# GpSimd finishes the normalised x of the plain feed-forwards, VectorE makes its low halves, and four pairs of columns run on the raw x in place of six

## The reference

```
def swiglu(x, w1, w3, w2):
    return (jax.nn.silu(x @ w1) * (x @ w3)) @ w2

x = layer_norm_2(DEEPNORM_ALPHA * x + mix, ln1_g[i], ln1_b[i])
x = layer_norm_2(DEEPNORM_ALPHA * x + swiglu(x, ffn_w1[i], ffn_w3[i], ffn_w2[i]), ln2_g[i], ln2_b[i])
```

## Time and profile before

| | |
|---|---|
| Median of three runs | 1377.0 us |
| The profiled execution | 1375.53 us |
| Its span, first to last instruction | 1373.7 us |
| TensorE matmul busy | 1355.4 us, 99% |
| VectorE busy | 978.7 us, 71% |
| ScalarE busy | 935.3 us, 68% |
| GpSimd busy | 423.4 us, 31% |
| Mean granted TensorE clock | 0.996 |

### The profile page before, as it was taken

How to read it: one execution, slowest core, us unless ns; L and a number is a source line. 1 busy time by engine, 2 the same in 40 slices (tenths; PEclk the granted TensorE clock), 3 DMA queues, 4 the chain that set the end, 5 groups by cost and what they waited for, 6 DMA issues and landing times.

```text
span 1373.7 us, 30422 instructions
## 1 busy us (share of the span) xinstructions
PE 1355.4 (99%) x11052; PEld 1320.7 (96%) x11052; DVE 978.7 (71%) x1523; ACT 935.3 (68%) x1597; POOL 423.4 (31%) x426
## 2 busy tenths in 40 slices
PE   9999999999999999999999999999999999999998
PEld 8899889999999999999999889999998989999998
DVE  7867776886548878875579868554587876855457
ACT  5633447756876577666977868457877897755876
POOL 3343002432203335322146028332044402632203
PEclk9999999999999999999999999999999999999999
DMA  5532205556564564565645235655644614666562
GB/s 212 175 116 92 86 32 183 168 184 200 177 196 157 183 203 137 181 200 191 198 157 187 74 128 170 209 192 167 215 151 150 216 61 153 208 193 194 186 201 93
DMA packets 63166, 225.74 MB, mean 164 GB/s; under 512 B 7008, under 2 KB 8416, under 8 KB 63072
## 3 DMA queue, kind: packets, MB, share of 16 engines
q1 hardware_dynamic: 62064, 221.47, 50.3%
q10 hardware_dynamic: 1008, 3.01, 0.6%
HBM read 223.40 MB, written 1.05 MB: 163 GB/s over the span
## 4 chain that ended last, share of the span: by engine, by line
PE 82%; DVE 9%; ACT 5%; issue 2%; DMA 1%; POOL 0%; SPq 0%; DVEq 0%; ACTq 0%; POOLq 0%
PE bank L486 21%; PE bank L487 21%; PE bank L507 15%; PE bank L615 6%; DVE w_lo_space L1970 2%; ACT w_hi_space L1285 1%; PE bank L535 1%; PE bank L549 1%; PE bank L523 1%; DVE both L2074 1%; PE bank L481 1%; PE bank L483 1%; PE bank L482 1%; PE bank L1027 1%; PE bank L1020 1%
## 5 line engine op out<-in xcount | busy, mean ns | idle before, releaser
L1970 DVE TENSOR_TENSOR w_lo_space<-raw,w_hi_space 128x1024 fp32r<-128x1024 f32 x294 | 381.5, 1305 | 99.5 <-ACT w_hi_space L1285 92.0
L1285 ACT ACTIVATE w_hi_space<-raw 128x1024 fp32r<-128x1024 f32 x298 | 312.3, 1052 | 80.9 <-PE bank L507 50.5
L486 PE MATMUL bank<-x_hi,w_hi_space 128*128 128x262 f32 (+6 forms) x1144 | 286.4, 287 | 0.5 <-DVEq L2077 0.5
L487 PE MATMUL bank<-x_lo,w_hi_space 128*128 128x262 f32 (+6 forms) x1144 | 283.1, 284 | 0.0
L1968 DVE SCALAR_TENSOR_TENSOR w_lo_space<-raw,negmean,w_hi_space 128x1024 fp32r<-128x1024 f32 x120 | 158.0, 1317 | 145.4 <-ACT w_hi_space L1283 145.0
L486 PEld LDWEIGHTS bank<-x_hi,w_hi_space 128*128 128x128 f32 x1144 | 216.9, 190 | 1.9 <-issue 1.1
L487 PEld LDWEIGHTS bank<-x_lo,w_hi_space 128*128 128x128 f32 x1144 | 217.0, 190 | 0.3
L486 PE MATMUL bank<-x_space,w_hi_space 128*128 128x256 f32 (+3 forms) x896 | 214.9, 280 | 0.0
L487 PE MATMUL bank<-x_space,w_hi_space 128*128 128x256 f32 (+3 forms) x896 | 214.1, 280 | 0.0
L2884 POOL TENSOR_TENSOR a_space<-av,a_space 128x256 fp32r<-128x256 f32 (+1 forms) x88 | 99.5, 1131 | 309.0 <-ACT a_space L1543 124.5
L486 PEld LDWEIGHTS bank<-x_space,w_hi_space 128*128 128x128 f32 x896 | 169.2, 189 | 0.1
(11 more groups left out here) (516 smaller groups left out, 2691.8 us busy)
## 6 DMA issues: line engine op xcount, KB each, us to landing
raw<-w SPq DMA_DIRECT2D x418, 512.0 KB, 3.8
h<-h SPq DMA_DIRECT2D x4, 272.0 KB, 3.8
out<-h SPq DMA_DIRECT2D x8, 128.0 KB, 1.9
T<-cs ACTq DMA_DIRECT2D x1, 960.0 KB, 6.4
con_b<-cb ACTq DMA_DIRECT2D x1, 712.0 KB, 6.1
con_g<-ca ACTq DMA_DIRECT2D x1, 421.5 KB, 6.2
p_raw<-pin ACTq DMA_DIRECT2D x1, 256.0 KB, 3.5
smx<-pin ACTq DMA_DIRECT2D x1, 256.0 KB, 6.4
```

The costliest lines, as they stand in the source:

```text
L486: pe.matmul(o, wh, xh, start=first, stop=False)
L487: pe.matmul(o, wh, xl, start=False, stop=False)
L1285: A(weights_of(s)[0][:, slot, :], raw[:, slot, :], ACT.Copy).then_inc(S("hi_ready"), 1)
L1970: V.tensor_tensor(wl[:, slot, :], raw[:, slot, :], wh[:, slot, :].bitcast(F32), ALU.subtract).then_inc(S("lo_ready"), 1)
```

## The change

`RAW_PAIRS` goes from 6 to 4. GpSimd no longer makes the low halves of the normalised x; it finishes `h` itself, with `keep` (a multiplication by `rstd`, a wait for its own result, then one instruction with gain and bias), for all eight tiles before it comes to the hidden values. ScalarE takes its rounded half as a plain copy of the finished `h`, two tiles in pair 0, three in pair 1, three in pair 2, and no longer makes the full one. VectorE makes the low halves, in the same places, behind the `av` of the pair. The feed-forwards with a convolution keep their code. `keep` was in the program and is:

The diff:

```
--- before.py
+++ after.py
@@ -82,7 +82,7 @@
 
 X2_STEP = KT * SEQ
 
-RAW_PAIRS = 6
+RAW_PAIRS = 4
 RAW_CONV = 10
 
 NEXT_LINE = [U["up2"] + 2 * RAW_PAIRS, U["up3"] + 2 * RAW_PAIRS, U["m_out"]]
@@ -345,6 +345,10 @@
         def x2_low(i, k):
 
             return x2[:, k, halves_x[i]:2 * halves_x[i]] if i < 2 else x2_late[1][:, k, :]
+
+        def late_tiles(j):
+
+            return (range(0, 2), range(2, 5), range(5, 8))[j] if j < 3 else ()
 
         def a_tile(i, part, j, n):
 
@@ -1588,7 +1592,10 @@
                     act.wait_ge(S("unit_done"), u + 2)
                     ahead(u + 1, s + 1)
                     if conv is None:
-                        tiles = range(2 * j, min(2 * j + 2, KT))
+                        for k in late_tiles(j):
+                            act.wait_ge(S("ln_h"), KT * 2 * ups[0] + k + 1)
+                            A(x2_high(ups[0], k), h[:, k, 0:N], ACT.Copy).then_inc(S("x2_hi"), 1)
+                        tiles = ()
                     else:
                         tiles = range(2) if j == 0 else range(j + 1, min(j + 2, KT))
                     for k in tiles:
@@ -2428,6 +2435,10 @@
 
                     dve.wait_ge(S("a_ready"), j + (base + 1))
                     V.scalar_tensor_tensor(out=av[:, par, 0:M], in0=gate[:, N - M:N], scalar=gate[:, N:N + 1], in1=sl[:, par, 0:M], op0=ALU.add, op1=ALU.mult).then_inc(S("ffn_product"), 1)
+                    if conv is None:
+                        for k in late_tiles(j):
+                            dve.wait_ge(S("x2_hi"), KT * ups[0] + k + 1)
+                            V.tensor_tensor(x2_low(ups[0], k), h[:, k, 0:N], x2_high(ups[0], k).bitcast(F32), ALU.subtract).then_inc(S("x2_ready"), 1)
 
                 one_over(2 * ups[0], N)
                 if conv is None:
@@ -2865,7 +2876,8 @@
                     centre(c, j, N)
 
             def low_parts(i, n, N, M):
-                kept[0] += 1
+                if i < 2:
+                    kept[0] += 1
 
                 def times(k):
                     G.tensor_tensor(h[:, k, 0:N], r[:, k, 0:N], rstd[:, 0:N], ALU.mult).then_inc(S("ln_h1"), 1)
@@ -2875,17 +2887,18 @@
                     pool.wait_ge(S("ln_h"), KT * n + k + 1)
                     G.tensor_tensor(x2_low(i, k), h[:, k, 0:N], x2_high(i, k).bitcast(F32), ALU.subtract).then_inc(S("x2_ready"), 1)
 
-                for k in range(KT if i >= 2 else KT // 2):
-                    times(k)
+                if i < 2:
+                    for k in range(KT // 2):
+                        times(k)
+                else:
+                    for k in range(KT):
+                        keep(n, k, N)
                 for j in range(FT):
                     if j == KT:
                         pool.wait_ge(S("ln_h"), KT * (n + 1))
                     pool.wait_ge(S("a_hi"), j + (i * FT + 1))
                     G.tensor_tensor(a_tile(i, 1, j, M), av[:, j % 2, 0:M], a_tile(i, 0, j, M).bitcast(F32), ALU.subtract).then_inc(S("a_ready"), 1)
-                    if i >= 2:
-                        for k in range(2 * j, min(2 * j + 2, KT)):
-                            low_half(k)
-                    else:
+                    if i < 2:
                         for k in range(2) if j == 0 else range(j + 1, min(j + 2, KT)):
                             low_half(k)
                         if j < KT // 2:
```

## The result

The changed kernel takes 1386.9 us (median of 6 runs, 1384.7 to 1390.7) against 1377.3 us before (median of 6): 1.0072 of the time, 95% interval 1.0054 to 1.0089. It is slower, by 9.6 us. The profiled execution took 1388.09 us, 12.56 us more than its counterpart before.

A forecast was written before the change was run, and what follows sets the result against it. TensorE was taken to bound plain feed-forwards throughout. Each loses 4.9 (wait) + 1.8 (clock) - 0.72 (shorter units) = 6.0 us, together 12.0; 1375.53 profiled becomes 1387.5, plus 1.5 for the median: 1389.0 us, range 1381 to 1398.

The forecast's parts named there:

- The chain that sets the border: Raw to normalised x: GpSimd's eight tiles, hidden tile 0's low half, VectorE's `av`, three low halves; TensorE waits until 853.1.
- Its length: TensorE's wait at the border between raw and normalised x, from 848.2 to 853.1: 4.9 us per feed-forward.
- GpSimd's eight tiles: GpSimd finishing h: 12.9 us alone plus 5.6 us of contention with VectorE, 18.5 us, last tile at 850.3.
- The links behind: After the last tile of h: hidden low half 0.74 us, release and `av` 0.9, three low halves of 0.41.
- The clock: TensorE's granted clock falls to 1.2 GHz behind the wait in each feed-forward, costing 1.8 us each, ends 0 and 3.2.
- The saving: TensorE's up-projection: 4 units per feed-forward take 2.72 us in place of 2.90, 0.72 us less.
- No wait: Rival at the border: all eight low halves in place by 848.17, only shorter units left; 1375.6 us, chance 0.05.
- VectorE's floor: Rival: VectorE's list, not GpSimd, sets the border; wait 2.2 us, 1380 to 1383.6 us in all, chance 0.18.
- Full contention: Rival: GpSimd suffers fully from VectorE in the raw pairs; wait 8.9 us, 1398 us in all, chance 0.13.

The follow-up runs named there:

- e3: Changed kernel with GpSimd making hidden tile 0's low half after its fourth tile of h, not its eighth; 1385.82 us, 1.0069 of the kernel before.
- e5: Changed kernel, but ScalarE finishes h again (rounded half and full value) and GpSimd only multiplies by rstd; 1383.28 us, 1.0054 of the kernel before.
- e9: Changed kernel, reordered only: hidden tile 0's low half after GpSimd's fourth tile, low halves of tiles 5 to 7 ahead of `av`; 1379.55 us, 1.0033 of before.
- e6: Changed kernel, ScalarE finishing tiles 0 to 4, GpSimd 5 to 7, low halves of 5 to 7 ahead of `av`; 1375.62 us, 0.9987 of before.
- e10: The kernel of e6 once more, beside the kernel before; 1374.99 us, 0.9999 of the kernel before.
- e7: The changed kernel as it is, measured and profiled again; 1388.67 us, 1.0086 of the kernel before.
- e2: The kernel before with RAW_PAIRS 4 in place of 6 and no other edit; 1395.44 us, 1.0136 of the kernel before.
- e4: Changed kernel with TensorE running 16 small matmuls on zeros ahead of its wait at the border; 1387.29 us, 1.0078 of the kernel before.
- e8: The kernel of e4 once more, beside the changed kernel on the same chip; 1385.91 us, 1.0062 of the kernel before.

## Why the prediction was right

The forecast was 1389.0 us in a range of 1381 to 1398, with the sign; it measured 1386.9. The mechanism was right; that the sum came so near to the trace is partly luck, as the last but one point says. By its steps:

- **The chain that sets the border** was right, link by link, and e3, e5 and e9 showed each link: the buffer of `av` alone 1.1 us (e3), the buffer and GpSimd's scale-and-shifts together 2.0 us (e5). The two orders together leave 1.5 us (e9), and with the work divided otherwise as well nothing is left (e6).
- **Its length** was 3.85 us, not 4.9. The mis-sized term is GpSimd's eight tiles: from 832.56 to 849.61 they took 17.05 us, not 18.5. The scale-and-shift takes 0.55 us alone, not 0.71, and the wait between the two is 0.10 us, not 0.17. The 0.71 was a misreading: that instance ran from 717.80 to 718.51 us, beside an instruction of VectorE on two arrays. The contention that I spread over both instructions fell on the scale-and-shift here, as its 16 instances show (min/median/max in ns, first line), against the multiplication (second line):
```profile
L2850 POOL TENSOR_SCALAR h<-h,prm x16: 548/1114/2464, 833.5 to 1184.8; 128x256 f32<-128x256 f32 x16
L2848 POOL TENSOR_TENSOR h<-both,rstd x16: 728/732/838, 832.6 to 1184.0; 128x256 f32<-128x256 f32 x16
```
  The eight in the first feed-forward add up to 10.5 us where alone they would be 4.4: 6.1 us of stretching, for which I had 5.6. With 8 x (0.73 + 0.10 + 0.55) = 11.0 in place of 12.9 that gives the 17.1.
- **The links behind** took 0.70 us for the hidden low half (I had 0.74), 0.86 for `av` with its release (0.9), and 1.55 for the three low halves (1.2): 0.3 us too short in all, which took back a part of the error in GpSimd's tiles.
- **The clock** fell in both feed-forwards, as expected, and cost 1.6 us in the first (100.2 against 98.6), where I had 1.8. That it is so near is luck: 1.8 was picked between 0 and 3.2, and in the first feed-forward of e3 a fall cost 2.8 (101.4 against 98.6).
- **The saving** of the shorter units: e6 and e10, which have it without a wait, show 0.9 us per feed-forward; I had 0.72.
- **What I did not have** is the pace of 2.83 us per unit, 2.8 us in the profiled execution (103.0 against 100.2). In that execution it made up for the waits, which were 2.1 us shorter in sum than forecast: my sum was 12.0, the trace's 12.4, and the agreement is luck. The medians differ by 9.6 us. That the long units are missing in some of those runs would fit, but no trace shows it.
- **The rivals.** No wait: what e6 reached, with the division of work and the order both changed. VectorE's floor: seen in e5. Full contention: did not happen: in the first feed-forward the scale-and-shifts took 1.31 us on average and the multiplications 0.74, where this rival had 1.43 and 0.98.

## What to carry to other kernels

When a step is moved to an idle engine, write down that engine's list behind the step as well: of 3.85 us of wait, 1.1 came from one small instruction queued behind it, whose result another chain's buffer needed. An earlier hand-over that gains 0.18 us per unit moves its deadline by whole units (11.6 us for 0.7 us gained), so read the slack at the old deadline first; here it was 2.9 us.

## What the runs showed of the hardware

- **GpSimd beside VectorE.** A one-array scale-and-shift of 128 x 256 took 0.55 us while VectorE was idle, and 2.46 us where VectorE made two weight halves from two SBUF arrays each. It did not slow VectorE: the weight half beside it took 1.21 us, and a pair takes 2.36 with GpSimd idle. The half that began during a multiplication (two arrays) of GpSimd took 1.57 us. In the changed kernel, first feed-forward:
```profile
838.35 0.73 POOL L2848 TENSOR_TENSOR h<-both,rstd 128x256 f32<-128x256 f32 x1
839.18 2.46 POOL L2850 TENSOR_SCALAR h<-h,prm 128x256 f32<-128x256 f32 x1
838.60 1.57 DVE L1977 TENSOR_TENSOR w_lo_space<-raw,w_hi_space 128x1024 fp32r<-128x1024 f32 x1
840.09 1.21 DVE L1977 TENSOR_TENSOR w_lo_space<-raw,w_hi_space 128x1024 fp32r<-128x1024 f32 x1
```
  But a multiplication can be held up too. In this feed-forward only the first of the eight began during a weight half, 0.2 us before its end, and took 0.79 us; the others began right behind a scale-and-shift, which had taken the delay. In the kernel before one began 0.08 us behind the start of a weight half and took 1.75 us in place of 0.73, and the next weight half took 1.76:
```profile
837.89 1.75 POOL L2871 TENSOR_TENSOR h<-both,rstd 128x256 f32<-128x256 f32 x1
838.95 1.76 DVE L1970 TENSOR_TENSOR w_lo_space<-raw,w_hi_space 128x1024 fp32r<-128x1024 f32 x1
```
  The page GPSIMD Engine Reference of the Trainium skill (1. Specifications) says that GpSimd's SBUF interface is shared with VectorE, and that contention comes with VectorE instructions that have two SBUF inputs. The traces agree: these are the instructions beside which GpSimd's times grew.
- **The clock and short waits.** At the border the granted clock fell to 1.2 GHz behind every wait of 1.82 us and longer (e5, e3, the changed kernel and e7, e2: ten waits), and stayed at 2.4 behind 1.50 and 1.46 us (e9) and where small matmuls filled the wait (e4, e8: four waits). The wait of 1.8 us for `yp_lo` at about 1040 us brought a fall in eleven of twelve traces and none in e9. What decides in such a case is open.
- **A third pace.** At the full clock the same 24 matmuls took 2.83 us in place of 2.72: in 2 of the 10 plain feed-forwards in which the clock had fallen at the border (the changed kernel, e7), up to the next plain float32 matmul, and in none of the 14 in which it had not. But a fall of the clock is not needed for it, since the mixer's units at 735 to 744 us have it in all twelve traces. What chooses it is open.
